# Smaller first pieces, VectorE's weight splits behind the softmax scaling, ScalarE's copies of turned probabilities ahead of the squares: a two-layer encoder trunk on one core

## The reference: what is computed

```
for each of DEPTH = 2 layers:
    h = rms_norm(x) * norm_w
    p = h @ w_in                       # 2048 -> 5824 columns, split among all branches
    A: differential attention          # 4 heads, two softmax maps each, q/k norm, partial rotary
    B: grouped-query attention         # 4 query heads, 2 key/value heads, q/k norm, 2-D rotary
    C: latent attention                # low-rank q and kv: rms_norm, then @ w_uq, @ w_ukv
    D: pooling mixer                   # centred means minus token, 128x128 matrix per group
    every branch output * silu(its gate columns of p)
    x = x + concat(A, B, C, D) @ w_out # 2048 x 2048
drop the meta tokens
```

## Time and profile before

| what | us |
|---|---|
| median of 3 runs (lowest to highest) | 904.98 (904.94 to 906.03) |
| the profiled execution, its own time | 905.02 |
| its span | 903.2 |
| TensorE busy (matmul) | 895.9 (99%) |
| VectorE busy | 639.5 (71%) |
| ScalarE busy | 566.5 (63%) |
| mean granted TensorE clock | 0.999 of full speed |
| weights read from HBM | 140.58 MB, 158 GB/s over the span |

### The profile page before, as it was taken

One profiled execution on the slowest core, in us unless ns is written; L12 is line 12 of the kernel. 1 busy time (PEld: TensorE's weight loads), 2 busy tenths in 40 slices (PEclk: granted clock), 3 DMA queues, 4 the chain that ended last, 5 costly groups with the idle time before them and its releaser, 6 DMA issues.

```text
span 903.2 us, 18071 instructions
## 1 busy us (share of the span) xinstructions
PE 895.9 (99%) x7070; PEld 860.0 (95%) x7070; DVE 639.5 (71%) x1074; ACT 566.5 (63%) x986; POOL 0.2 (0%) x4
## 2 busy tenths in 40 slices
PE   8999999999999999999999999999999999999998
PEld 7999998998999999999999999999999999999998
DVE  7785887778777776766665659887687667766552
ACT  7678756577666667745454588556686666665331
POOL 0000000000000000000000000000000000000000
PEclk9999999999999999999999999999999999999999
DMA  8754333343434443445455544334435344445561
GB/s 333 264 197 140 134 140 137 124 136 115 145 139 143 139 149 130 147 147 190 172 199 186 188 176 151 118 120 176 149 97 184 140 141 157 152 158 187 187 217 64
DMA packets 22996, 143.83 MB, mean 159 GB/s; under 512 B 2560, under 2 KB 4736, under 8 KB 6528
## 3 DMA queue, kind: packets, MB, share of 16 engines
q1 hardware_dynamic: 22768, 142.64, 44.4%
q10 hardware_dynamic: 144, 0.04, 0.1%
HBM read 140.58 MB, written 2.10 MB: 158 GB/s over the span
## 4 chain that ended last, share of the span: by engine, by line
PE 97%; ACT 1%; DMA 1%; SPq 0%; DVE 0%; issue 0%; ACTq 0%; DVEq 0%
PE dense L736 27%; PE dense L738 26%; PE dense L737 26%; PE s_ps L907 4%; PE o_ps L943 4%; PE norm_ps L862 2%; PE t_ps L922 2%; DMA raw<-w_stream_dram 1%; ACT w_hi L1039 1%; PE swap_ps L738 0%; PE norm_ps L738 0%; PE norm_ps L737 0%; PE swap_ps L737 0%; PE swap_ps L736 0%; PE norm_ps L736 0%; PE norm_ps L951 0%
## 5 line engine op out<-in xcount | busy, mean ns | idle before, releaser
L736 PE MATMUL dense<-h_hi,w_hi 128*128 128x272 f32 (+2 forms) x1440 | 427.1, 297 | 2.3 <-DVE h_lo L1328 2.3
L738 PE MATMUL dense<-h_hi,w_lo 128*128 128x272 f32 (+2 forms) x1440 | 412.7, 287 | 0.0
L737 PE MATMUL dense<-h_lo,w_hi 128*128 128x272 f32 (+2 forms) x1440 | 410.9, 285 | 0.0
L1348 DVE TENSOR_TENSOR w_lo<-raw,w_hi 128x1024 fp32r<-128x1024 f32 (+1 forms) x256 | 312.0, 1219 | 86.5 <-ACT w_hi L1039 80.3
L1039 ACT ACTIVATE w_hi<-raw 128x1024 fp32r<-128x1024 f32 (+1 forms) x256 | 270.3, 1056 | 70.4 <-PE dense L738 56.1
L736 PEld LDWEIGHTS dense<-h_hi,w_hi 128*128 128x128 f32 x1440 | 271.3, 188 | 7.9 <-issue 2.8
L737 PEld LDWEIGHTS dense<-h_lo,w_hi 128*128 128x128 f32 x1440 | 271.4, 188 | 1.2
L738 PEld LDWEIGHTS dense<-h_hi,w_lo 128*128 128x128 f32 x1440 | 271.1, 188 | 0.0
L736 PE MATMUL dense<-y_hi,w_hi 128*128 128x272 f32 (+1 forms) x500 | 143.6, 287 | 0.2
L738 PE MATMUL dense<-y_hi,w_lo 128*128 128x272 f32 (+1 forms) x500 | 142.7, 285 | 0.0
L737 PE MATMUL dense<-y_lo,w_hi 128*128 128x272 f32 (+1 forms) x500 | 142.4, 285 | 0.0
(11 more groups left out here) (175 smaller groups left out, 808.1 us busy)
## 6 DMA issues: line engine op xcount, KB each, us to landing
raw<-w_stream_dram SPq DMA_DIRECT2D x128, 1024.0 KB, 4.8
out_dram<-x SPq DMA_DIRECT2D x8, 256.0 KB, 4.7
x<-xt_dram SPq DMA_DIRECT2D x3, 544.0 KB, 8.9
raw<-w_stream_dram SPq DMA_DIRECT2D x3, 512.0 KB, 7.6
con<-consts_dram SPq DMA_DIRECT2D x1, 984.0 KB, 7.8
x<-xt_dram SPq DMA_DIRECT2D x2, 272.0 KB, 4.8
raw<-w_stream_dram SPq DMA_DIRECT2D x2, 256.0 KB, 4.6
d_w<-consts_dram SPq DMA_DIRECT2D x2, 256.0 KB, 5.3
```

Source lines behind the costliest of these rows:

```text
L736: nc.tensor.matmul(ps, whi, xhi, start=first, stop=False)
L737: nc.tensor.matmul(ps, whi, xlo, start=False, stop=False)
L738: return nc.tensor.matmul(ps, wlo, xhi, start=False, stop=last)
L1348: signal(nc.vector.tensor_tensor(w_lo[:, g % RING, 0:n], raw[:, e % RAW, CHUNK * half:CHUNK * half + n], w_hi[:, g % RING, 0:n].bitcast(F3 ...
```

## The change

It has three parts.

1. **The start.** `FIRST` cuts the first chunk in pieces of 256, 256 and 512 columns (they go with x tile 0, x tile 1, x tiles 2 and 3). The x tiles 0 to 3 are loaded through ScalarE's queue, in three DMAs around that of `par`, instead of through SyncE's. `x_first` works two tiles at a time for tiles 4 to 7, and tiles 6 and 7 come behind the split of chunk 2.
2. **VectorE's splits.** For chunks 27 to 94 of each layer, VectorE's part of the split moves from place 0.71 of its slot to 0.521 of the next slot, right behind `s_scale` (0.491). ScalarE's part stays.
3. **ScalarE's `p_out`** moves from place 0.56 to 0.105 of its slot: ahead of `rope_pre` (0.11), `xscale` (0.283), `sub_pre` (0.439) and `x_out` (0.55).

```
+FIRST = [(0, 1), (1, 2), (2, 4)]
...
-                 y_split=0.66, xscale=0.283, sub_pre=0.439, x_out=0.55, p_out=0.56, gate=0.65, s_exp=0.579,
+                 y_split=0.66, xscale=0.283, sub_pre=0.439, x_out=0.55, p_out=0.105, gate=0.65, s_exp=0.579,
...
+LATE_SPLITS = (27, 95)
...
-            plan.append((slot + at_engine[kind] + MOVED.get(stage, 0), len(plan), stage))
-
-    for n in (0, 1):
-        plan += [(-11, 2 * n, ("split_half", n)), (-11, 2 * n + 1, ("x_half", n))]
+            place = at_engine[kind] + MOVED.get(stage, 0)
+            if kind == "split" and at_engine is AT_VECTOR and LATE_SPLITS[0] <= stage[2] < LATE_SPLITS[1]:
+                place = 1 + at_engine["s_scale"] + 0.03
+            plan.append((slot + place, len(plan), stage))
+
+    for n in range(len(FIRST)):
+        plan += [(-11, 2 * n, ("split_part", n)), (-11, 2 * n + 1, ("x_part", n))]
...
-    plan += [(-5, 0, ("x_first", 0, 1)), (-3, 0, ("x_first", 0, 2)), (2.9, 0, ("x_first", 0, 3))]
+    plan += [(-6.5, 0, ("x_first", 4, 6)), (-5, 0, ("x_first", 6, 8)), (-3, 0, ("x_first", 8, 12)),
+             (2.9, 0, ("x_first", 12, 16))]
...
-        for n in (0, 1):
-            at = slice(CHUNK // 2 * n, CHUNK // 2 * n + CHUNK // 2)
-            sp.dma_start(raw[:, 0, at], w_stream[0, :, at]).then_inc(s_first[0] if n else s_half, 16)
-            sp.dma_start(x[:, 2 * n:2 * n + 2, :], xt[:, 2 * n:2 * n + 2, :]).then_inc(s_x[0] if n else s_x_half, 16)
+        for n, (a, b) in enumerate(FIRST):
+            at = slice(256 * a, 256 * b)
+            sp.dma_start(raw[:, 0, at], w_stream[0, :, at]).then_inc((*s_part, s_first[0])[n], 16)
...
+            act.dma_start(x[:, 0:1, :], xt[:, 0:1, :]).then_inc(s_x_part[0], 16)
             act.dma_start(par[:, :], params).then_inc(s_par, 16)
+            act.dma_start(x[:, 1:2, :], xt[:, 1:2, :]).then_inc(s_x_part[1], 16)
+            act.dma_start(x[:, 2:4, :], xt[:, 2:4, :]).then_inc(s_x[0], 16)
             nc.scalar.preload_act_table_set("natural_log_exp_and_others")
```

More of the change, by code:

```diff
@@ L373, in build @@
     s_first = [sem(f"s_first{i}") for i in range(4)]
-    s_half, s_x_half = sem("s_half"), sem("s_x_half")
-    half_hi, half_lo, warm_zero = sem("half_hi"), sem("half_lo"), sem("warm_zero")
+    s_part, s_x_part = [sem("s_part0"), sem("s_part1")], [sem("s_x_part0"), sem("s_x_part1")]
+    part_hi, part_lo, warm_zero = sem("part_hi"), sem("part_lo"), sem("warm_zero")
     second_hi, second_lo = sem("second_hi"), sem("second_lo")
@@ L792, in first_chunk @@
             for k in range(CK):
-                if k == 0:
-                    pe.wait_ge(half_lo, 1)
-                if k == CK // 2:
+                if k < 2:
+                    pe.wait_ge(part_lo, k + 1)
+                if k == 2:
                     pe.wait_ge(lo_ready, 1)
@@ L976, in setup, with split_part @@
         def setup(_):
+            act.dma_start(x[:, 0:1, :], xt[:, 0:1, :]).then_inc(s_x_part[0], 16)
             act.dma_start(par[:, :], params).then_inc(s_par, 16)
+            act.dma_start(x[:, 1:2, :], xt[:, 1:2, :]).then_inc(s_x_part[1], 16)
+            act.dma_start(x[:, 2:4, :], xt[:, 2:4, :]).then_inc(s_x[0], 16)
             nc.scalar.preload_act_table_set("natural_log_exp_and_others")
[L980 to L983, removed]
+        def split_part(n):
+            at = slice(256 * FIRST[n][0], 256 * FIRST[n][1])
+            act.wait_ge((*s_part, s_first[0])[n], 16)
+            signal(nc.scalar.activation(w_hi[:, 0, at], raw[:, 0, at], ACT.Copy), part_hi if n < 2 else hi_ready,
+                   (1, 2, 1)[n])
         def second_half(n):
@@ L989, in second_half, with x_part, x_first @@
             signal(nc.scalar.activation(w_hi[:, 1, at], raw[:, 0, of], ACT.Copy), (second_hi, hi_ready)[n], 1 + n)
-        def x_half(n):
+        def x_part(n):
             if n == 0:
                 act.wait_ge(s_par, 16)
-            act.wait_ge((s_x_half, s_x[0])[n], 16)
-            for kt in (2 * n, 2 * n + 1):
+            act.wait_ge((*s_x_part, s_x[0])[n], 16)
+            for kt in range(*FIRST[n]):
                 x_hi(0, kt)
-        def x_first(_, c):
-            act.wait_ge(s_x[c], 16)
-            for kt in range(4 * c, 4 * c + 4):
+        def x_first(a, b):
+            act.wait_ge(s_x[a // 4], 16)
+            for kt in range(a, b):
                 x_hi(0, kt)
@@ L1222, in p_out @@
             signal(nc.scalar.activation(p_t[0:32, 4, at_q:at_q + nq], turned_tails(b, nq), ACT.Copy), pt_ready, k + 1)
-        run = dict(setup=setup, split_half=split_half, second_half=second_half, x_half=x_half, lift=lift, x_first=x_first, x_square=x_square, lam_exp=lambda_exp,
+        run = dict(setup=setup, split_part=split_part, second_half=second_half, x_part=x_part, lift=lift, x_first=x_first, x_square=x_square, lam_exp=lambda_exp,
                    x_out=x_out, split=split,
@@ L1258, in setup, with split_part @@
             nc.vector.memset(odd_only[0:16, :], 0.0).then_inc(tails_zero, 1)
-        def split_half(n):
-            at = slice(CHUNK // 2 * n, CHUNK // 2 * n + CHUNK // 2)
-            dve.wait_ge((half_hi, hi_ready)[n], 1)
+        def split_part(n):
+            at = slice(256 * FIRST[n][0], 256 * FIRST[n][1])
+            dve.wait_ge(part_hi if n < 2 else hi_ready, (1, 2, 1)[n])
             signal(nc.vector.tensor_tensor(w_lo[:, 0, at], raw[:, 0, at], w_hi[:, 0, at].bitcast(F32), ALU.subtract),
-                   (half_lo, lo_ready)[n], 1)
+                   part_lo if n < 2 else lo_ready, (1, 2, 1)[n])
         def second_half(n):
@@ L1270, in second_half, with x_part, x_first @@
                    (second_lo, lo_ready)[n], 1 + n)
-        def x_half(n):
+        def x_part(n):
             if n == 0:
                 dve.wait_ge(s_par, 16)
-            dve.wait_ge((s_x_half, s_x[0])[n], 16)
-            for kt in (2 * n, 2 * n + 1):
+            dve.wait_ge((*s_x_part, s_x[0])[n], 16)
+            for kt in range(*FIRST[n]):
                 x_lo(0, kt)
-        def x_first(_, c):
-            dve.wait_ge(s_x[c], 16)
-            for kt in range(4 * c, 4 * c + 4):
+        def x_first(a, b):
+            dve.wait_ge(s_x[a // 4], 16)
+            for kt in range(a, b):
                 x_lo(0, kt)
@@ L1526, in s_scale @@
             signal(last, w_ready, k + 1)
-        run = dict(setup=setup, split_half=split_half, second_half=second_half, x_half=x_half, x_first=x_first, x_add=x_add, lam_dot=lam_dot, lam_out=lam_out,
+        run = dict(setup=setup, split_part=split_part, second_half=second_half, x_part=x_part, x_first=x_first, x_add=x_add, lam_dot=lam_dot, lam_out=lam_out,
                    x_out=x_out, split=split, rescale=rescale, sq_sum=sq_sum, rope_mid=rope_mid, rope_turn=rope_turn, rope_fin=rope_fin,
```

## The result

| | us |
|---|---|
| before, median (6 runs) | 905.05 (904.94 to 906.03) |
| after, median (6 runs) | 910.58 (909.4 to 911.82) |
| ratio, with its 95% interval | 1.0061 [1.0048, 1.0074] |
| after, profiled execution: own time, span | 909.40, 907.6 |

The change makes the kernel slower by 0.6%. I had forecast 905.9 and no measurable change, so the forecast is wrong, outside its range. The profiled executions differ by 909.40 - 905.02 = 4.38 us. (The medians differ by more, 5.5. Executions far above the rest of their kernel, as one of 1452 us of `e1_start_only`, are left out of the ratios and counts.)

The account below looks back on a forecast made before the run. TensorE, busy 99% of the span, was taken as the bound. From 905.02 us, less 1.05 (start), 0.21 (head_out) and 0.54 (p_out), plus 2.68 (four late chunks), gave 905.90; range 903.2 to 907.1.

Parts of the forecast that it names:

- the landing of chunk 2 stays at about 11.1: At the start: x tiles in ScalarE's queue bring no bandwidth, so chunk 2's weights still land at about 11.1 us.
- the forecast -1.05 at chunk 3: At the start: TensorE starts chunk 3 at 16.69 instead of 17.75, 1.05 us gained.
- the start gives nothing: Rival, 10%: par lands late, ScalarE copies chunk 2 at 12.35, chunk 3 stays at 17.75; time 906.95 us.
- is worth nothing: At the start: chunk 0 starting half a microsecond sooner gains nothing, since chunk 1 ends before 13.57 either way.
- after chunk 3 nothing waits until the latents: After the start: the latents' waits hang on TensorE's own results and move with it, so the 1.05 us gain is kept.
- chunk 79: Layer 1: the moved split ends behind the rotation, at 745.59, so TensorE starts late; 1.35 us lost.
- chunk 61: Layer 0: VectorE has no gap, the split moves behind the scaling and ends at 233.36; 0.82 us lost.
- chunk 88: Layer 0: the split ends at 332.66 against 332.40, with the squares delayed 0.95 by the p_out move; 0.29 us lost.
- chunk 71: Layer 1: the split ends where the rotation did, 717.10 against 716.80; 0.22 us lost.
- head_out: A split goes out from ahead of this VectorE stage, which ended late once before turning matmuls; 0.21 us gained.
- Part 3: p_out's move: copies end sooner, so the product with the values after chunk 85 starts without waiting; 0.54 us gained.
- for some sum that is late by a tenth: Upper bound, 0.3 us, on the cost of the squares ending 0.95 later through p_out's move; taken as nothing.

Follow-up runs that it names:

- e1_start_only: The changed kernel with VectorE's splits and p_out put back, so only the start edits stay: 907.61 us, ratio 1.0026 to before.
- e10_best: The kernel before with the new order of tiles 4 to 7 and p_out at 0.105, nothing else: 903.73 us, ratio 0.9987.
- e7_tile_order_only: The kernel before with only x_first's work on tiles 4 to 7 in pairs, 4 and 5 ahead of chunk 2's split: 904.17 us, ratio 0.999.
- e5_pieces_x_on_sync: The kernel before with the smaller first pieces and new tile order, x staying on SyncE's queue: 906.79 us, ratio 1.0019.
- e6_halves_x_on_scalar: The kernel before, old halves and tile order, with x tiles 0 to 3 moved to ScalarE's queue around par: 907.04 us, ratio 1.0022.
- e2_splits_only: The kernel before with only VectorE's splits moved: 907.63 us, ratio 1.0026.
- e4_splits_and_pout: The kernel before with VectorE's splits and p_out moved, without the start edits: 907.65 us, ratio 1.0026.
- e8_four_splits_back: The kernel before with splits and p_out moved, except the splits of chunks 61 and 88 (layer 0), 71 and 79 (layer 1): 906.65 us, ratio 1.0016.
- e3_pout_only: The kernel before with only p_out moved from 0.56 to 0.105: 904.78 us, ratio 0.9995.

## Why the prediction was wrong

**The step that failed: the landings in part 1.** I wrote that "the landing of chunk 2 stays at about 11.1", put ScalarE's condition down to `par` alone, and took all tiles of x after the first as there in time. Chunk 2's weights landed at 12.4 (issued at 3.05, 9.4 to landing) and, what counted more, the tiles of x at 7.7 and 9.6, with ScalarE waiting for both. Three things took the place of the forecast -1.05 at chunk 3:

- The order of the tiles does give the 1.05. In `e10_best` chunk 2 starts at 13.54 and chunk 3 at 16.66; forecast were 13.63 and 16.69. (`e7_tile_order_only`, whose profiled execution lacks the p_out move, has 0.87.)
- ScalarE reached its copy of chunk 2 at 13.27 instead of 11.18, **+2.09**. The working forecast 5.75 us of ScalarE's work from the first tile on; it took 5.70. Adding the two waits for x gives 5.51 + 5.70 + 1.27 + 0.79 = 13.27. `e5_pieces_x_on_sync` and `e6_halves_x_on_scalar` show that both edits bring this about: with smaller pieces the transfers from x tile 1 on land later, and the second queue changes which bytes come first.
- The clock. VectorE had w_lo of chunk 2 ready at 15.67, so TensorE could have started at 15.73, but was still at chunk 1 and started at 16.40: **+0.67**. The low clock is enough for it: the last half of chunk 0 and the step to chunk 1 took 13.38 - 11.03 = 2.35; in the trace of before the same twelve matmuls took 10.65 - 9.07 = 1.58.

Together -1.05 + 2.09 + 0.67 = 1.71; measured 1.67. The rival "the start gives nothing" named the right place, ScalarE's copy of chunk 2, but for a wrong reason (`par`), and it ended too soon: its 12.35 was an end set by one transfer, where every transfer was in question. That chunk 0 starting sooner "is worth nothing" is true in this trace: its 0.33 are gone at chunk 1. Whether the sooner start also brought the clock down is not shown: in `e6_halves_x_on_scalar` chunk 0 started later than before and the clock fell as well. The run without that clock (`e5_pieces_x_on_sync`, granted clock 1.00 from 9 to 13, although it too paused) keeps +1.0 at chunk 3 from the data alone.

The rule of the Trainium skill that I quoted (page "DMA: Bandwidth & Descriptors", section "Issuing engines are not separate DMA queues") says that issuing from a second engine saves only the time of issue. The trace agrees in that the second queue brought no bandwidth: from 7 to 9 us the stream moves 397 GB/s after, 419 before. My conclusion from it, that the landing of chunk 2 stays, does not follow. The same page of the Trainium skill, section "Queues, rings and completion order", says that each DMA engine takes turns between the queues it has work for, a packet at a time. By that a queue with small packets would get the smaller share of the bytes. Rows that bear on it are the queues on the profile's page of `e6_halves_x_on_scalar`, in packets, MB and share:

```profile
q1 hardware_dynamic: 22480, 142.08, 44.0%
...
q10 hardware_dynamic: 432, 0.60, 0.2%
```

ScalarE's queue (q10) has packets of 1.4 KB in the mean, SyncE's (q1) of 6.3 KB over the whole run; and 272 KB of x landed at 10.0 there, behind a 512 KB chunk that was issued at the same time. That is consistent with turns by packet, if the profile's packets are those in which the turns are taken; no run isolates it.

**Part 2 was right in its places, a little small in its sizes.** Forecast and measured: chunk 79, 1.35 and 1.37; chunk 61, 0.82 and 0.96 (the sum left out the 0.06 from the end of a split to TensorE's start, which it had counted at chunk 79); chunk 88 (by my count; 87), 0.29 and 0.33; chunk 71, 0.22 and 0.26. Sum 2.68 and 2.92. `head_out`, 0.21 and 0.20. That chunk 87 is late only with p_out moved, as forecast ("part 3 delays the squares"), is shown by its absence in `e2_splits_only` and its presence in `e4_splits_and_pout`. That a split goes into the row and one goes out, which kept the scaling at chunk 61 in time, is shown by `e8_four_splits_back`, where none goes out.

**Part 3 was right.** Forecast 0.54, measured 0.54 in `e3_pout_only` and 0.55 in the changed kernel. Its bound of 0.3 "for some sum that is late by a tenth" became 0.17 at chunk 42 of layer 1.

The body thus cost 2.92 + 0.17 - 0.20 - 0.55 = 2.34 against the forecast 1.93; the start 1.67 against -1.05; and 0.25 at chunk 16 was not forecast: "after chunk 3 nothing waits until the latents, whose waits hang on TensorE's own results" overlooked that chunk 16 waits for VectorE's `y_lo`, with no slack. (Small drifts between the places make up the last 0.1 of the 4.38.) Of the error of 3.5 us in the profiled time, 2.7 are the start.

**What stays open.** Why small first pieces slow transfers that follow them and that have the same shape (335 against 402 GB/s in 9 to 11 us), and how much of the delay is only their number. What made ScalarE's gap of 0.28 at 35.14, from which the 0.25 at chunk 16 comes. What lets the clock fall in one execution of a kernel and not in the next. And why in `e6_halves_x_on_scalar` the executions with the lower mean clock are the faster ones.

## What to carry to other kernels

At a kernel's start, ask for each transfer when it lands under the new order and size of all transfers before it, not only for the one that is issued second; an order of instructions that fits the landings of today (here worth 0.9 to 1.1 us for one line of the table) need not be bundled with an edit that moves those landings. Where an engine has no gap, a moved instruction is one in and one out of a row, and taking back a single exchange makes the next chunk late instead. Starting the busiest engine sooner is no gain if it then pauses. And where a profile puts a short gap down to issue, look when each input of the waiting instruction was finished.

## What the runs showed of the hardware

- Smaller first pieces in one queue got the first bytes there sooner and the later ones later. In `e5_pieces_x_on_sync` ScalarE had its first weights at 3.49 instead of 5.08, but chunk 2's weights, in the same place of the queue but for two more small DMAs, at 13.19 instead of 11.18.
- The granted clock fell to the half level after TensorE had paused, in chunk 0 or (`e6_halves_x_on_scalar`) ahead of it, and stayed there for some 3.4 us in each of the four traces that show it. A pause need not bring it down: before had one of 1.69 us ahead of chunk 0, `e5_pieces_x_on_sync` one of 1.02 us in it, both with the clock at 1.00. Six executions of the changed kernel fall in two groups by mean clock: 0.998 with 909.4, 910.1 and 910.15; 0.996 with 911.01, 911.67 and 911.82. The medians of the groups are 1.6 us apart, for 0.002 of mean clock. That is less than half of why the median of all six, 910.58, lies above the profiled 909.40: the median of the 0.998 group is 910.1 already. It is no rule for other kernels: in `e6_halves_x_on_scalar` the order is the other way round.
